# Decoder step on one core: sample rows scaled on VectorE by a spread scale, vector transposes behind three token tiles, first banks in another order

## The reference, cut to what matters

```
x_prompt (1, 512, 1024), x_sample (8, 1, 1024), g_mix (1024)
xn = x * rsqrt(mean(x*x, over the 1024 channels) + 1e-6) * g_mix
u  = xn @ w_in        # 6144 columns, then the two branches, the FFN, the gates
```

## Time and profile before

| | |
|---|---|
| runs | 943.49, 942.68, 943.15 us, median 943.15 us |
| profiled execution | 943.24 us |
| span of that execution in the trace | 941.5 us |
| PE busy | 918.6 us (98%) |
| DVE busy | 524.1 us (56%) |
| ACT busy | 388.6 us (41%) |
| POOL busy | 235.7 us (25%) |

### The profile page before, as it was taken

The page is one execution under the profiler, slowest core; times in us unless marked ns, Lnnn a source line. Parts: engine busy times, 40 slices in busy tenths (PEclk is TensorE's granted clock), DMA queues, the critical chain, the costliest instruction groups (busy, mean ns, idle before and its releaser), DMA issues. The chain is left out here.

```text
span 941.5 us, 21025 instructions
## 1 busy us (share of the span) xinstructions
PE 918.6 (98%) x7964; PEld 904.2 (96%) x7964; DVE 524.1 (56%) x612; ACT 388.6 (41%) x518; POOL 235.7 (25%) x289
## 2 busy tenths in 40 slices
PE   7999999999999999999999999999999999999996
PEld 6999989999999999999999999999999999999995
DVE  5432258878655654666566556666655443434643
ACT  6322355465444544423345444444443221223433
POOL 0007057867410101001641111111111031212341
PEclk9999999999999999999999999999999999999998
DMA  6233533323334344533323333333233433332212
GB/s 221 70 90 90 180 92 90 85 71 89 89 112 119 106 125 142 177 116 98 91 68 104 96 91 89 89 89 89 89 89 100 121 93 92 92 90 63 85 56 91
DMA packets 176472, 94.74 MB, mean 101 GB/s; under 512 B 17888, under 2 KB 174960, under 8 KB 176016
## 3 DMA queue, kind: packets, MB, share of 16 engines
q1 hardware_dynamic: 149698, 80.61, 28.8%
q10 hardware_dynamic: 26736, 13.60, 5.1%
HBM read 86.25 MB, written 8.03 MB: 100 GB/s over the span
## 5 line engine op out<-in xcount | busy, mean ns | idle before, releaser
L1168 DVE TENSOR_TENSOR wlo<-raw,whi 128x1024 fp32r<-128x1024 f32 (+2 forms) x132 | 195.8, 1483 | 174.4 <-ACT whi L831 174.4
L831 ACT ACTIVATE whi<-raw 128x1024 fp32r<-128x1024 f32 (+2 forms) x132 | 146.7, 1111 | 353.4 <-PE acc L485 352.0
L485 PE MATMUL acc<-xah,whi 128*128 128x260 f32 x896 | 187.7, 291 | 0.0
L485 PE MATMUL acc<-xah,wlo 128*128 128x260 f32 x896 | 180.8, 283 | 0.0
L485 PE MATMUL acc<-xal,whi 128*128 128x260 f32 x896 | 180.5, 283 | 0.0
L485 PE MATMUL acc<-xbh,whi 128*128 128x260 f32 x816 | 165.3, 284 | 0.8 <-issue 0.8
L485 PE MATMUL acc<-xbh,wlo 128*128 128x260 f32 x816 | 164.4, 283 | 0.0
L485 PE MATMUL acc<-xbl,whi 128*128 128x260 f32 x816 | 164.2, 283 | 0.0
L485 PEld LDWEIGHTS acc<-xah,whi 128*128 128x128 f32 x896 | 138.6, 189 | 3.3 <-issue 1.9
L485 PEld LDWEIGHTS acc<-xal,whi 128*128 128x128 f32 x896 | 138.6, 189 | 0.0
L485 PEld LDWEIGHTS acc<-xah,wlo 128*128 128x128 f32 x896 | 138.4, 189 | 0.0
(11 more groups left out here) (286 smaller groups left out, 1194.7 us busy)
## 6 DMA issues: line engine op xcount, KB each, us to landing
raw<-in_w_in SPq DMA_DIRECT2D x96, 256.0 KB, 3.2
raw<-in_w_up SPq DMA_DIRECT2D x88, 256.0 KB, 3.1
raw<-in_w_down SPq DMA_DIRECT2D x16, 384.0 KB, 3.2
raw<-in_w_down SPq DMA_DIRECT2D x16, 320.0 KB, 3.7
raw<-in_w_out SPq DMA_DIRECT2D x16, 256.0 KB, 3.0
raw<-in_w_ple_gate SPq DMA_DIRECT2D x8, 512.0 KB, 3.7
x_transposed<-xstg SPq DMA_DIRECT2D x1, 2080.0 KB, 7.7
hT<-x_transposed ACTq DMA_DIRECT2D x1, 2080.0 KB, 8.3
```

Of the source, the lines that this page charges most:

```text
L485: mm = pe.matmul(sums[:, b, 0:HT], wt[slot][:, w], xx[:, c, b * HT:(b + 1) * HT], start=first and i == 0 and q == 0, stop=last and i == n ...
L831: act.activation(whi[k % 2][:, 0:n], raw[k % 2][:, 0:n], ACT.Copy).then_inc(hi_ready, 1)
L1168: dve.tensor_tensor(wlo[k % 2][:, 0:n], raw[k % 2][:, 0:n], whi[k % 2][:, 0:n].bitcast(fp), SUB).then_inc(lo_ready, 1)
```

## The change

- The sample scale is spread over the 128 partitions by a single matmul: `ones1024` (each element 1/1024, 8 rows of it) by `dg`, which is now multiplied by 1024 on its way. It stands in PE's stream right behind the raw rows. It replaces the eight matmuls of L534.
- DVE multiplies the spread scale by the raw sample columns, which lie in `xstg` already, and, once the vectors are there, by the gain. A new semaphore `xs_ready` tells ACT that `xsm` is done.
- The vector transposes go from ahead of all scaled transposes to a place behind token tiles 0 to 2. PE's wait for all nine vector loads goes with them.
- `x_bank` begins with `ob` and the two banks of `acc[1]`; the two banks of `lvb` are fourth and fifth. The wait for `lvb` stands ahead of these two alone.
- The three small steps of the lower bound go behind the eight instructions of L1223.

```diff
--- before.py
+++ after.py
@@ -271,6 +271,7 @@
         x_root = sem("x_root")
         x_scale = sem("x_scale")
         x_norm = sem("x_norm")
+        xs_ready = sem("xs_ready")
         x_diag = sem("x_diag")
         x_tile = sem("x_tile")
         xa_hi = sem("xa_hi")
@@ -360,7 +361,7 @@
 
         def x_bank(j):
 
-            return (lvb[:, 0, :], lvb[:, 1, :], ob[:], acc[1][:, 0, :], acc[1][:, 1, :])[j % 5]
+            return (ob[:], acc[1][:, 0, :], acc[1][:, 1, :], lvb[:, 0, :], lvb[:, 1, :])[j % 5]
 
         block = ctx.enter_context(nc.Block())
 
@@ -510,30 +511,30 @@
 
             for n in range(4):
                 raw_rows(n)
-            pe.wait_ge(vec_loaded, 16 * 9)
+
+            pe.wait_ge(x_diag, 1)
             pe.wait_ge(misc_free, 1)
-            pe.transpose(mb[:, 0:48], vrow[0:48, 0, :], ident[0:48, 0:48])
-            pe.transpose(mb[:, 48:136], vrow[0:88, 1, :], ident[0:88, 0:88]).then_inc(misc_full, 1)
-
-            for b in range(2):
-                pe.wait_ge(lv_free[b], 2)
+            pe.matmul(mb[:, 0:NS], ones1024[0:NS, :], dg[0:NS, 0:NS], start=True, stop=True).then_inc(misc_full, 1)
+
+            def vectors():
+                pe.wait_ge(vec_loaded, 16 * 9)
+                pe.wait_ge(misc_free, 2)
+                pe.transpose(mb[:, 0:48], vrow[0:48, 0, :], ident[0:48, 0:48])
+                pe.transpose(mb[:, 48:136], vrow[0:88, 1, :], ident[0:88, 0:88]).then_inc(misc_full, 1)
 
             def x_columns(i, j):
                 return pe.transpose(x_bank(j)[:, i * 128:(i + 1) * 128], xnr[:, i, j * 128:(j + 1) * 128], ident)
 
             for i in range(NCH):
+                if i == NCH - 1:
+                    vectors()
                 pe.wait_ge(x_norm, i + 1)
                 for j in range(5):
+                    if i == 0 and j >= 3:
+                        pe.wait_ge(lv_free[j - 3], 2)
                     mm = x_columns(i, j)
                     if i == NCH - 1:
                         mm.then_inc(x_tile, 1)
-                if i == 1:
-                    pe.wait_ge(x_diag, 1)
-                    pe.wait_ge(misc_free, 2)
-                    for q in range(DC):
-                        mm = pe.matmul(mb[:, q * 8:q * 8 + 8], xtok[0:NS, 4, q * 128:(q + 1) * 128],
-                                       dg[0:NS, 0:NS], start=True, stop=True)
-                    mm.then_inc(misc_full, 1)
             for j in range(5, DC):
                 pe.wait_ge(xa_lo, j - 5 + 2)
                 for i in range(NCH):
@@ -860,7 +861,7 @@
             act.dma_start(msk[:], masks).then_inc(const_loaded, 16)
             hi("A", 0, 0)
 
-            act.wait_ge(misc_free, 3)
+            act.wait_ge(xs_ready, 1)
             act.activation(xah[:, :, NT:TT], xsm[:], ACT.Copy).then_inc(xa_hi, 1)
             for j in range(DC):
                 act.wait_ge(x_tile, j + 1)
@@ -1197,7 +1198,7 @@
                     dve.tensor_scalar(xnr[:, i, :], xtok[:, i, :], ssx[:, i:i + 1], None, MUL).then_inc(x_norm, 1)
 
             token_scale(4, 0)
-            dve.tensor_scalar(dg[0:NS, 0:NS], ident[0:NS, 0:NS], ssx[0:NS, 4:5], None, MUL).then_inc(x_diag, 1)
+            dve.tensor_scalar(dg[0:NS, 0:NS], ident[0:NS, 0:NS], ssx[0:NS, 4:5], float(DM), MUL, MUL).then_inc(x_diag, 1)
             x_copy(0)
             token_scale(0, 1)
             x_copy(1)
@@ -1207,14 +1208,13 @@
             token_scale(2, 3)
             token_scale(3, 4)
             dve.wait_ge(misc_full, 2)
+            dve.tensor_tensor(xsm[:], mb[:, 0:NS].unsqueeze(1).broadcast_to([128, DC, NS]), xstg[:, :, NT:TT],
+                              MUL).then_inc(misc_free, 1)
+            dve.wait_ge(misc_full, 3)
             dve.tensor_copy(vc[:], mb[:, 0:136]).then_inc(misc_free, 1)
-            dve.wait_ge(misc_free, 2)
-            step(dve.tensor_tensor(lbt[:, 0, :], vc[:, 0:4], vc[:, 4:8], ALU.max))
-            step(dve.tensor_tensor(lbt[:, 1, :], vc[:, 0:4], lbt[:, 0, :], SUB))
-            dve.tensor_tensor(lbt[:, 2, :], vc[:, 4:8], lbt[:, 0, :], SUB).then_inc(vec_ready, 1)
-            dve.wait_ge(misc_full, 3)
-            dve.tensor_tensor(xsm[:], mb[:, 0:64].rearrange("p (a b) -> p a b", b=NS),
-                              vc[:, 8:16].unsqueeze(2).broadcast_to([128, DC, NS]), MUL).then_inc(misc_free, 1)
+            dve.wait_ge(misc_free, 3)
+            dve.tensor_tensor(xsm[:], xsm[:], vc[:, 8:16].unsqueeze(2).broadcast_to([128, DC, NS]),
+                              MUL).then_inc(xs_ready, 1)
             lo("A", 0, 0)
             dve.wait_ge(xa_hi, 1)
             dve.tensor_tensor(xal[:, :, NT:TT], xsm[:], xah[:, :, NT:TT].bitcast(fp), SUB).then_inc(xa_lo, 1)
@@ -1222,6 +1222,9 @@
                 dve.wait_ge(xa_hi, j + 2)
                 dve.scalar_tensor_tensor(xal[:, j, 0:NT], x_bank(j), vc[:, 8 + j:9 + j],
                                          xah[:, j, 0:NT].bitcast(fp), MUL, SUB).then_inc(xa_lo, 1)
+            step(dve.tensor_tensor(lbt[:, 0, :], vc[:, 0:4], vc[:, 4:8], ALU.max))
+            step(dve.tensor_tensor(lbt[:, 1, :], vc[:, 0:4], lbt[:, 0, :], SUB))
+            dve.tensor_tensor(lbt[:, 2, :], vc[:, 4:8], lbt[:, 0, :], SUB).then_inc(vec_ready, 1)
             lo("A", 1, 0)
             dve.wait_ge(lb_exp, 1)
             step(dve.tensor_tensor(lbt[:, 5, :], lbt[:, 1, :], lbt[:, 2, :], ADD))
```

## The result

The changed kernel takes 937.99 us in the median of five runs (936.62 to 938.35) against 942.85 us (942.49 to 943.49): ratio 0.9949, 95% interval 0.9939 to 0.996. It is 4.9 us or 0.5% faster. The forecast was 938.6 us. The profiled execution happened to be the fastest of the five, 936.62 us with a span of 934.8 us, so its trace has to be read with care: it is 6.6 us shorter than the profiled execution of before, 1.8 us more than the medians differ.

A forecast was written before the change was run, and what follows sets the result against it. PE, busy 98% of the span, was taken as the bound, its head setting when the matmul stream begins. 943.24 - 4.6 (3.9 spread and vectors, 0.7 ACT's wait) = 938.6 us; own range 937.6 to 939.6, full range 937.1 to 941.0 us.

The forecast's parts named there:

- The bound: PE is the limit; its waits behind the head are small, so a microsecond won before the first product arrives at the end.
- The head shift of 4.6 us: First L1223 on DVE moves from 19.90 to 15.3 us: 3.9 us from spread and vectors, 0.7 us from ACT's wait.
- ACT's wait of 0.7 us: DVE's 0.70 us wait for ACT's first L867 before the first L1223 disappears, as L867 starts at 14.3 us.
- a spread matmul of up to 1 us: Spread matmul behind the raw rows costs 0.45 us; any price from nothing to 1 us changes nothing that follows.
- The transposes of tiles 6 and 7: PE reaches these channel tiles at 16.9 and 17.7 us without waiting; the first product begins at 18.5 us.
- the small steps: Some 0.6 us on DVE, moved ahead of the second `wlo`, which ends at about 22.5 us, hidden by the first product.
- the cover: The first product, lasting until about 25.8 us, hides the second `wlo`; without it the moved steps would cost 0.6 us.
- The clock: The rise to 2.4 GHz follows the first product's start by 3.4 us, so the 4.6 us come through whole.
- Rival (b): Clock rises sooner after the first product begins, at best at once: 1.5 us more gain, 937.1 us; chance 6%.

The follow-up runs named there:

- b_fill: Kernel before plus five unread matmuls before the first transpose and four in the wait for the vectors: 939.19 us, ratio 0.9972.
- a_banks: Changed kernel with the old `x_bank` order and the wait for `lvb` ahead of j = 0 and 1: 938.95 us, ratio 0.9966.
- eight: Changed kernel with the eight sample matmuls in place of the one spread matmul, `dg` without its factor 1024: 940.75 us, ratio 0.9977.
- spread: Kernel before with only the spread matmul and two DVE multiplications replacing the eight matmuls and one, old places and banks: 938.29 us, ratio 0.995.
- a_thin: Changed kernel plus four unread matmuls of 8 moving columns in PE's idle time before channel tile 5's transposes: 937.61 us, ratio 0.9948.
- a_gap: Changed kernel plus four unread 128-column matmuls in PE's 2.0 us idle time before channel tile 5's transposes: 936.25 us, ratio 0.9942.
- a_again: The changed kernel run again without any edit, for a second trace and five more times: 938.31 us, ratio 0.9953.
- a_lb: Changed kernel with the three small lower-bound steps ahead of the multiplication by the gain again: 938.93 us, ratio 0.9959.
- a_early: Changed kernel plus only five unread 128x128 matmuls before the first transpose: 938.01 us, ratio 0.9953.

## Why the prediction was right

**The bound.** Right. PE's waits behind the head stayed as they were, and the rest behind the first product is 912.4 to 913.2 us in 13 of 14 traces, so what the head wins arrives at the end.

**The head shift of 4.6 us.** Right. Counted from the raw rows, the first L1223 came 4.9 and 4.7 us sooner in the two traces of the changed kernel, with the clock up early, and 4.4 to 4.5 us sooner in four variants with the lower level that the forecast assumed. ACT's wait of 0.7 us went as said. In absolute times all came 0.4 us later than said up to L1223 (13.94 for 13.5 us, 14.70 for 14.3 us, 15.69 for 15.3 us), since the second token tile landed later in that execution and held the raw rows up. PE's wait of 0.5 us for DVE before the vectors was not in the sum; it is there in the three traces whose clock was up early, so the faster transposes bring only 0.2 to 0.5 us at the first L1223. Two readings were wrong without consequence. The first L867 had waited for the first of the five transposes of token tile 3, not the last. And a spread matmul of up to 1 us would have changed what follows, as the forecast itself has no wait at token tile 2 (11.75 us, with its rows ready at 10.92 us), so any delay of PE would go on; it took 0.5 us, as summed.

**The transposes of tiles 6 and 7, and the small steps.** Right: no wait in them, and the second `wlo` ends at 22.64 us (22.5 us said) with the first product running until 24.0 us. It ended earlier than assumed, and the cover left was 1.4 us, not 3.3 us.

**The clock.** This step failed: "the rise follows the product, 3.4 us behind it, since transposes from 11.35 us on did not bring it". In ten of the eleven traces of the changed kernel and its variants, and in `b_fill`, the upper level came while PE worked on transposes, between 8.2 us (`a_banks`) and 18.4 us (`eight`), in the changed kernel itself at about 11.2 us and, in its second trace, by 8.6 us. The Trainium skill's statement, "TensorE: Matmul & The Clock Gate", Part 4, that the full clock does not engage for transposes is contradicted for these float32 transposes. What Part 1 of the same page says, that the moment moves between executions of one kernel, is what the two traces of the changed kernel show (11.2 us, then by 8.6 us and again at 18.9 us). That the number came out near all the same is partly luck: in four of the five traces of this head with the hole open, the early rise was followed by a fall in or behind the hole, so that the product took 6.1 to 7.1 us. That is closer to the 7.4 us of before, kept by the forecast, than the 5.8 us of the upper level. Rival (b) had the time of the profiled execution (936.62 us for 937.1 us), but not its reason, since the rise came 7 us ahead of the product; the median of the five is in the forecast's own range.

**What stays open.** When the clock rises in an execution was not steered, only shifted in its odds. `spread` and the full change have the same time within their scatter of 1 us, while the head differs by 0.9 to 1.4 us; the larger hole is the likely reason, but `spread` with a filled hole was not tried. So the gain of the second half is shown in the head and not in the device time. How much L534's kind of matmul does for the clock was not settled by `a_thin`.

## What to carry to other kernels

In a kernel whose PE is busy throughout, look at what stands ahead of the first dense stretch. Many small matmuls that do a scaling can be one matmul and an elementwise product, and a wait for many small loads belongs as late as its result allows. After such a gain look at the hole that opens on PE: here four useless matmuls in it brought about another microsecond, `a_gap` with 936.25 us having the lowest median. Compare distances between events inside one trace, not absolute times, and don't read one trace as the typical one where the clock decides a microsecond.

## What the runs showed of the hardware

- The clock's level can rise during float32 transposes. At about 11.2 us their distance went from 0.21 to 0.11 us each, and in `a_again` PE had done nothing but transposes when they took 0.65 us for four at 8.62 us. The distance of 260-column matmuls is 0.22 and 0.12 us in the two levels.
- It also falls again. It did so inside an idle stretch of PE in `a_again` (15.5 us, idle for 2.04 us), `a_banks` (14.9 us, 2.04 us) and `a_lb` (17.4 us, 2.50 us), behind shorter ones in `a_thin`, `a_early` and `eight` (1.2 to 1.7 us), and in `b_fill` half a microsecond behind the eight matmuls of 8 columns.
- The granted clock column shows such a fall as 0.50 (`a_again`, 15.5 to 18.9 us). Before the first rise of an execution it reads 1.00 although the pace is the lower one (up to 26.5 us before), and there only the distance between matmuls shows the level.
- The head's transfers vary: PE waited 1.14 us for the second token tile in the changed kernel's first trace, 1.44 us in `eight`, and not at all before, and the vectors let the old order go on at 11.35 us before, 11.69 us in `spread` and 10.76 us in `b_fill`.
